# FFN down projection by seven products of halves (Strassen) in place of eight, in blocks of 512 features

## Chip, core and metric

The kernel runs on one core of one Trainium2 chip. The metric is device time in microseconds of one execution, lower is better; three runs of the kernel before are shown. The engines are TensorE (PE in the rows; PEld is its weight load), VectorE (DVE), ScalarE (ACT), GpSimd (POOL) and SyncE (SP), which here issues the loads and stores.

## What is computed

One step of a decoder layer for a prompt of 1024 tokens and 32 sample tokens, D_MODEL 1024, D_FF 4096: a combined input projection, three groups of heads (dilated attention, mLSTM, HGRN2), an output projection, an MLP and a final norm. The change is in the MLP:

```
x = x + mix.astype(x.dtype) @ w_out
u = rmsnorm(x, g_ffn) @ w_up
x = x + jnp.square(jax.nn.relu(u)) @ w_down
...
y = rmsnorm(x, g_final)
```

All matrices are float32. Where the kernel wants float32 accuracy from TensorE it splits each operand into a high part (rounded to the engine's fp32r format by a copy on ACT) and a low part (the operand less its high part), and adds three products: low × high, high × low, high × high. The helper `product` (lines 340 to 342) issues the three matmuls for each slice of 128 of the contraction.

## The kernel before

The program is written by hand engine by engine in phases (a, b, c, e, f1, f2, g). What an engine does, and in which order, is the order of the code; engines meet at semaphores, each with a running count. Phase g is the MLP after its norm. x1 holds the running sum in SBUF (eight tiles of 128 prompt tokens and one tile for the sample tokens), XH and XL the normalised and transposed input in two parts.

Phase g before runs over 16 blocks (NBLK) of 256 features (NF = 2 slices of 128):

- `hidden_piece`: six up pieces per block. A piece is one slice of 128 features by a third of the tokens (TG = 352 columns), 8 slices of the contraction × 3 = 24 matmuls of 352 columns.
- Relu on DVE (line 2496), square (2452) and high part (2454) on ACT, low part (2486) on DVE: UH and UL.
- Down: 16 products (8 token tiles × 2 halves of the output columns), each 2 slices × 3 = 6 matmuls of 512 columns into one of four PSUM banks, and one product for the sample tokens (`product_by_columns`, line 350, from raw float32). DVE adds each to x1 (line 2506).
- Weights: SP loads pieces of 512 KB (line 2087), ACT makes the high part (2091), DVE the low part (2095). POOL has nothing to do in phase g.

At the start of phase g, DVE waits for `x1_in`, which counts the loads of g_final among others: SP issues one load of g_final for the prompt (line 2379) and four small ones for the sample tokens (2381), then the weights. In the last block the tiles are finished one after the other: `final(i)` (lines 2476 to 2481) takes ACT's sum of squares and square root, a reciprocal and one pass over the tile on DVE, then SP stores it (2387). Pieces 0 and 1 of the first block are already done in phase f2; the first pieces' PSUM banks let PE do two more before it needs the first relu.

Of the kernel before, what the change touches and what calls it, by code (L numbers as in the profile page):

```python
# [39 lines left out]
P = 128  # L40
D = 1024
# [110 lines left out]
def program(nc, i_, o_):  # L152

    ctx = ExitStack()
    with ctx:
# [78 lines left out]
        R_up = [place("R_up0", 12288, 4096, F32R), place("R_up1", 16384, 4096, F32R)]  # L234
        R_down = place("R_down", 0, 4096, F32R)
        R_stage = place("R_stage", 4096, 2048)
        R_upos = place("R_upos", 7168, 704)
        R_raw = [place(f"R_raw{n}", at, 1024) for n, at in enumerate((6144, 8576, 9600, 10624))]
        R_ur = place("R_ur", 11648, 2 * NS)
        R_xr = place("R_xr", 51840, KD * NS)  # L240
        R_usq = place("R_usq", 7872, 704)
        R_u = place("R_u", 47616, 4224, F32R)
# [3 lines left out]
        R_junk = place("R_junk", 12288, 1024)  # L246
# [1584 lines left out]
        def phase_e_sync(sp):  # L1831
            load_key_chunks(sp, (6,))
            load_caches(sp, (6, 7))
            stream_values(sp)
            sp.wait_ge(ov_psum, 1)
            load_chunks(sp, 0, KD)
# [215 lines left out]
        FB = 256  # L2052
        NF = FB // P
        NBLK = DFF // FB
        wup = i_["w_up"][0].rearrange("(c k p) n -> c p k n", k=4, p=P)
# [7 lines left out]
        UP_CHUNKS, DOWN_CHUNKS = {}, {}  # L2063
        for b in range(NBLK):
            UP_CHUNKS[b] = len(CHUNKS)
            for c in range(2):
                high = 2048 * c
                CHUNKS.append((at(R_up[b % 2], high), at(R_up[b % 2], high + 1024), wup[c, :, :, b * FB:(b + 1) * FB],
                               at(R_stage, c * 1024) if b else at(R_first, c * 1024)))
            DOWN_CHUNKS[b] = len(CHUNKS)  # L2070
            for f in range(NF):
                high = 2048 * f
                CHUNKS.append((at(R_down, high), at(R_down, high + 1024), wdn[NF * b + f],
                               R_raw[2 * (b % 2) + f]))
        chunk_in = [sem(f"chunk_in{n}") for n in range(8)]
        d_psum = sem("d_psum")
        ND = 2 * NCH + 1
        def load_chunks(sp, first, last):
            for m in range(first, last):
                b, n = divmod(m - UP_CHUNKS[0], 4)  # L2080
                if n < 2 and b >= 2:
                    sp.wait_ge(chunk_split, NW + m - 3)
                if n >= 2 and b >= 2:
                    sp.wait_ge(d_psum, ND * (b - 1))
                src = CHUNKS[m][2]
                dst = CHUNKS[m][3] if len(src.shape) == 2 else CHUNKS[m][3].rearrange("p (k n) -> p k n", k=src.shape[1])
                sp.dma_start(dst, src).then_inc(chunk_in[m % 8], 16)
# [200 lines left out]
        def phase_f2_act(act):  # L2288
            for i in range(NTILE + 2):
# [8 lines left out]
                if i >= 2:  # L2298
# [6 lines left out]
                    if j in (3, 5):  # L2305
                        chunk_high_part(act, UP_CHUNKS[0] + j // 4)

        def phase_f2_dve(dve):
# [12 lines left out]
            for i in range(NTILE + 2):  # L2321
# [11 lines left out]
                if i >= 2:  # L2333
# [65 lines left out]
        def u_bank(U):  # L2399
            return U + 4 if U < 2 else U % 4  # L2400
# [178 lines left out]
```

## Time and profile before

| | |
|---|---|
| runs, us | 1560.49, 1556.29, 1560.10 |
| median, us | 1560.1 |
| profiled execution, span from first to last instruction, us | 1556.7 |
| busy in the span, us | PE 1498.3, PEld 1318.1, DVE 852.5, ACT 479.9, POOL 206.3 |
| phase g, us of the span | from about 812 to the end |
| granted TensorE clock, mean | 0.990 |

The span stands beside the runs' times: the profiled execution's span is 3.4 us under their median; no other time is given for that execution. Busy is the time in which an engine has an instruction in work. PE's matmuls overlap one another, so its busy time is longer than the pitch at which they follow. The granted clock is a share of 2.4 GHz; 0.50 is the lower level, 1.2 GHz.

### The profile page before, as it was taken

The numbers are of one execution on the slowest core, as the hardware profiler recorded it, in microseconds if no ns is written. First come the engines' busy times: TensorE is split into PE (matmuls) and PEld (weight loads), VectorE is DVE, ScalarE is ACT, GpSimd is POOL, SyncE is SP. The second block draws the span as 40 slices with busy tenths as digits, with TensorE's granted clock in tenths as the row PEclk, the third lists the DMA queues.
The fourth block names the chain that finished last, engine by engine and source line by source line (L and its number), as shares of the span: only waits on it lengthen the run. The fifth ranks groups of instructions, "written<-read, shape, count | busy, mean of one in ns | idle before, by whom it ended". The sixth has DMA issues, their size and how long they took to land.

```text
span 1556.7 us, 27891 instructions
## 1 busy us (share of the span) xinstructions
PE 1498.3 (96%) x11634; PEld 1318.1 (85%) x11634; DVE 852.5 (55%) x1729; ACT 479.9 (31%) x943; POOL 206.3 (13%) x298
## 2 busy tenths in 40 slices
PE   6999999999998998989999999999999999999997
PEld 4989899899996666858888899988899988899986
DVE  6864554668844777653455544444544444544446
ACT  6343222232213676432222222121222121222123
POOL 2212222889400000013000000000000000000000
PEclk9999999999998999999999999999999999999999
DMA  7422105522128412882103011111011111011102
GB/s 204 161 54 45 39 8 99 83 72 58 54 66 317 172 58 68 309 320 69 33 21 133 28 42 41 55 55 55 27 41 41 55 54 55 28 41 42 54 1 112
DMA packets 104559, 127.24 MB, mean 82 GB/s; under 512 B 26611, under 2 KB 78647, under 8 KB 103539
## 3 DMA queue, kind: packets, MB, share of 16 engines
q1 hardware_dynamic: 102370, 120.74, 24.9%
q0 software_dynamic: 2064, 4.72, 0.8%
q8 instruction: 93, 1.52, 0.4%
q14 instruction: 32, 0.25, 0.1%
HBM read 111.17 MB, written 18.98 MB: 84 GB/s over the span
## 4 chain that ended last, share of the span: by engine, by line
PE 89%; DVE 5%; ACT 2%; issue 2%; DMA 1%; SPq 1%; POOL 0%; DVEq 0%; ACTq 0%
PE PS L340 22%; PE PS L342 22%; PE PS L341 21%; PE PS L1644 2%; PE PS L1665 2%; PE PS L2204 2%; PE PS L2206 2%; PE PS L2205 2%; PE PS L1684 2%; PE PS L1918 2%; PE PS L350 1%; PE PS L1928 1%; PE PS L1484 1%; DVE R_att L1747 1%; DMA R_cache<-in_cache_attn_v 1%
## 5 line engine op out<-in xcount | busy, mean ns | idle before, releaser
L340 PE MATMUL PS<-x_high,R_up 128*128 128x352 f32 x768 | 249.6, 325 | 0.6 <-DVE R_upos L2496 0.6
L2506 DVE TENSOR_TENSOR R_x<-R_x,PS 128x512 f32<-128x512 f32 (+1 forms) x272 | 182.0, 671 | 123.7 <-PE PS L342 117.9
L342 PE MATMUL PS<-x_high,R_up 128*128 128x352 f32 x768 | 247.7, 322 | 0.0
L341 PE MATMUL PS<-x_low,R_up 128*128 128x352 f32 x768 | 246.8, 321 | 0.0
L2452 ACT ACTIVATE R_usq<-R_upos 128x352 f32<-128x352 f32 x96 | 47.8, 498 | 552.4 <-issue 365.1
L340 PE MATMUL PS<-R_down,R_u 128*128 128x512 f32 x512 | 202.2, 395 | 0.5 <-DVE R_u L2486 0.5
L342 PE MATMUL PS<-R_down,R_u 128*128 128x512 f32 x512 | 201.6, 394 | 0.0
L341 PE MATMUL PS<-R_down,R_u 128*128 128x512 f32 x512 | 201.1, 393 | 0.0
L2496 DVE TENSOR_SCALAR R_upos<-PS 128x352 f32<-128x352 f32 x96 | 50.3, 525 | 247.9 <-PE PS L342 242.8
L340 PEld LDWEIGHTS PS<-x_high,R_up 128*128 128x128 f32 x768 | 144.1, 188 | 7.0 <-issue 7.0
L341 PEld LDWEIGHTS PS<-x_low,R_up 128*128 128x128 f32 x768 | 144.7, 188 | 0.0
L342 PEld LDWEIGHTS PS<-x_high,R_up 128*128 128x128 f32 x768 | 144.5, 188 | 0.0
L340 PE MATMUL PS<-xn_high,R_w 128*128 128x352 f32 x384 | 126.6, 330 | 3.1 <-ACT R_hscr L730 2.0
L341 PE MATMUL PS<-xn_low,R_w 128*128 128x352 f32 x384 | 123.8, 322 | 2.0 <-issue 2.0
L340 PE MATMUL PS<-R_w,xn_low 128*128 128x256 f32 x432 | 125.5, 291 | 0.0
L342 PE MATMUL PS<-xn_high,R_w 128*128 128x352 f32 x384 | 124.1, 323 | 0.0
L341 PE MATMUL PS<-R_w,xn_high 128*128 128x256 f32 x432 | 122.7, 284 | 0.0
L342 PE MATMUL PS<-R_w,xn_high 128*128 128x256 f32 x432 | 122.2, 283 | 0.0
L342 PEld LDWEIGHTS PS<-R_down,R_u 128*128 128x128 f32 x512 | 96.1, 188 | 22.8
L340 PEld LDWEIGHTS PS<-R_down,R_u 128*128 128x128 f32 x512 | 96.1, 188 | 22.5 <-issue 1.2
L341 PEld LDWEIGHTS PS<-R_down,R_u 128*128 128x128 f32 x512 | 96.3, 188 | 21.8
L601 POOL TENSOR_TENSOR R_w<-R_wstage,R_w 128x1024 fp32r<-128x1024 f32 x29 | 74.8, 2582 | 174.6 <-ACT R_w L596 174.6
(390 smaller groups left out, 2613.1 us busy)
## 6 DMA issues: line engine op xcount, KB each, us to landing
R_raw<-in_w_down SPq DMA_DIRECT2D x32, 512.0 KB, 4.3
R_stage<-in_w_up SPq DMA_DIRECT2D x30, 512.0 KB, 3.8
R_wstage<-in_w_in SPq DMA_DIRECT2D x28, 512.0 KB, 4.3
R_cache<-in_cache_attn_v SPq DMA_DIRECT2D x56, 256.0 KB, 9.2
R_cache<-in_cache_attn_k SPq DMA_DIRECT2D x28, 256.0 KB, 5.9
R_cache<-in_cache_attn_k SPq DMA_DIRECT2D x7, 1024.0 KB, 9.4
bias_by_distance_copies<-bias_by_distance POOLq DMA_DIRECT2D x1, 4608.0 KB, 27.8
queries_and_keys<-R_spill SPq DMA_DIRECT2D x24, 176.0 KB
```

Source lines behind the costliest of these rows:

```text
L340: pe.matmul(out, ll, rh, start=(k == 0), stop=False)
L341: pe.matmul(out, lh, rl_, start=False, stop=False)
L342: mm = pe.matmul(out, lh, rh, start=False, stop=(k == n - 1))
L601: pool.tensor_tensor(parts_at(m)[1], wst[stage_of[m]], parts_at(m)[0].bitcast(F32), ALU.subtract)\
L1644: mm = pe.matmul(PS[:, 2 * h2 + c // 512, 0:min(512, nk - c)], aqk[part, hp, i * P:(i + 1) * P], aqk[part, 4 + hp, c:min(c + 512, nk)], st ...
L1665: t = pe.transpose(PS[:, 4 + gid % 2, (k - k0) * P:(k - k0 + 1) * P], PB[(2 * p + h2) % 6][:, k * P:(k + 1) * P], ident[:, :])
L1684: mm = pe.matmul(PS[64 * h2:64 * h2 + 64, 6 + p % 2, 0:P], va[:, k, 2 * hp + h2, 0:E], PT[h2][:, k, :], start=(k == 0), stop=(k == i))
L1918: t = pe.transpose(PS[:, b, a * P:(a + 1) * P], cache[4 * g + b][k][:, a * P:(a + 1) * P], ident[:, :])
L2204: pe.matmul(out, XL[:, k, ts], WOH[:, k, ns], start=(k == 0), stop=False)
L2452: act.activation(u_sq[U % 2], u_pos[U % 2], ACT.Square).then_inc(u_squared, 1)
L2496: dve.tensor_scalar(u_pos[U % 2], PS[:, u_bank(U), 0:TG], 0.0, None, ALU.max).then_inc(u_relu, 1)
L2506: dve.tensor_tensor(part, part, PS[:, 4 + j % 4, 0:w], ALU.add).then_inc(d_taken, 1)
```

## The change

The down projection of a block is done by Strassen's scheme in Winograd's form: the token halves, the feature halves and the output column halves make 2 × 2 matrices of quarters, and seven products of quarters (or of sums of quarters) take the place of eight. For that, a block has 512 features (NF = 4, NBLK = 8): twelve up pieces, the sample's product over four slices, then seven steps P1, P2, P6, P7, P5, P3, P4. A step multiplies a left operand (512 tokens × 256 features) by a right one (256 features × 512 columns): four products of six matmuls. Some steps add to a bank that holds an earlier one (P6 on P1, P7 on P6, P3 on P5), and DVE adds each product to one or two of x1's quarters (`ADDED_TO`), 32 additions of 512 columns per block.

The operands: `LEFT` and `RIGHT` name them. Sums of quarters (S_1, S_3, S_4 on the left, T_1 to T_4 on the right) are made in place, by POOL; s2 by DVE. ACT makes all high parts, DVE the left low parts and P6's right one, POOL the other right low parts and those of the up weights. There are two buffers of each operand (`ua`, `wb`). U and the raw weights stay in float32 in SBUF.

```
-        FB = 256
-        NF = FB // P
-        NBLK = DFF // FB
+        NF = 4
+        NUP = DFF // P
+        NBLK = NUP // NF
...
+        P1, P2, P6, P7, P5, P3, P4 = STEPS = range(7)
+        LEFT = {P1: q11, P2: q12, P6: s2, P7: q21, P5: q11, P3: q12, P4: q22}
+        RIGHT = {P1: w11, P2: w21, P6: t2, P7: w12, P5: w11, P3: w22, P4: w21}
+        OPENS = (P1, P2, P5, P4)
+        SECOND_BANKS = (P2, P5, P3)
+        ADDED_TO = {P1: [(0, 0)], P2: [(0, 0)], P6: [(0, 1)], P7: [(1, 0), (1, 1)], P5: [(1, 1)], P3: [(0, 1)], P4: [(1, 0)]}
...
+        def operand_free(eng, b, k):
+
+            G = 7 * b + k
+            if G >= 2:
+                pb, pk = divmod(G - 2, 7)
+                eng.wait_ge(d_psum, product_index(pb, pk, 3) + 1)
...
+            load_chunk(sp, KD + 2)
+            load_chunk(sp, KD + 3)
+            raw_rows(0, 0)
+            raw_rows(0, 1)
             for j in range(4):
                 sp.dma_start(g_sample[32 * j:32 * j + 32],
...
+            def step(b, k):
+                pe.wait_ge(dve_split, dve_count(b, k, "right" if k == P6 else "left"))
+                if k != P6:
+                    pe.wait_ge(right_split, 6 * b + POOL_LOWS.index(k) + 1)
+                (uh, ul), (wh, wl) = ua[(7 * b + k) % 2], wb[(7 * b + k) % 2]
+                for p in range(4):
+                    if k == P1 and p == 3:
+                        pe.wait_ge(d_taken, ND * b + 1)
+                    elif k == P1 and b:
+                        pe.wait_ge(d_taken, product_index(b - 1, P4, p) + 1)
+                    if k == P2:
+                        pe.wait_ge(u_relu, NU * b + NU - 3 + p)
+                    if k in (P6, P7, P5, P3, P4):
+                        pe.wait_ge(d_taken, product_index(b, {P6: P1, P7: P6, P5: P2, P3: P5, P4: P7}[k], p) + 1)
+                    out, ts = PS[:, product_bank(k, p), :], slice(p * P, (p + 1) * P)
+                    for f in range(2):
+                        pe.matmul(out, ul[:, f, ts], wh[:, f, :], start=(f == 0 and k in OPENS), stop=False, skip_group_check=True)
+                        pe.matmul(out, uh[:, f, ts], wl[:, f, :], start=False, stop=False, skip_group_check=True)
+                        mm = pe.matmul(out, uh[:, f, ts], wh[:, f, :], start=False, stop=(f == 1), skip_group_check=True)
+                    mm.then_inc(d_psum, 1)
...
+                pool.wait_ge(d_psum, ND * b + 1)
+                pool.wait_ge(right_split, 6 * b + POOL_LOWS.index(P2) + 1)
+                pool.tensor_tensor(w11, w12, w11, ALU.subtract).then_inc(pool_sums, 1)
+                pool.wait_ge(pool_sums, sums_count(b, T_1))
+                pool.tensor_tensor(t2, w22, w11, ALU.subtract).then_inc(pool_sums, 1)
+                pool.tensor_tensor(w12, w22, w12, ALU.subtract).then_inc(pool_sums, 1)
+                pool.wait_ge(pool_sums, sums_count(b, T_2))
+                pool.tensor_tensor(w21, w21, t2, ALU.subtract).then_inc(pool_sums, 1)
+                pool.wait_ge(s2_ready, b + 1)
+                pool.wait_ge(dve_split, dve_count(b, P2, "left"))
+                pool.tensor_tensor(q11, q11, s2, ALU.add).then_inc(pool_sums, 1)
+                right_low_part(b, P7)
+                pool.tensor_tensor(q12, q12, s2, ALU.subtract).then_inc(pool_sums, 1)
+                right_low_part(b, P5)
+                if not last:
+                    up_low(NF * b + 6)
+                right_low_part(b, P3)
+                right_low_part(b, P4)
...
-            dve.wait_ge(x1_in, 16 * 18)
+            dve.wait_ge(x1_in, 16 * 17)
...
+                for p in range(4):
+                    added(b, P4, p)
+                    if last:
+                        if p == 0:
+                            dve.wait_ge(x1_in, 16 * 18)
+                        final(LAST_TILES[p])
+            for i in LAST_TILES[4:]:
+                final(i)
```

`right_low_part(b, k)` on POOL waits for ACT's high part of the same operand and subtracts it; `left_low_part` does the same on DVE. `added(b, k, p)` waits for the product and adds it. The load of g_final for the prompt now goes out after the last up piece.

SP at the start of phase g: SP's rows before, from the loads of phase f2 on. R_row and R_x take g_final, R_raw w_down, R_stage w_up.

```order
L2236 DMA R_x<-in_c_token_sum 128x128
L2238 DMA R_x<-in_x_sample 32x256 x4
L2379 DMA R_row<-in_g_final 128x1024 [waits norm_split,op_psum]
L2381 DMA R_x<-in_g_final 32x256 x4
L2087 DMA R_raw<-in_w_down 128x1024 x2
L2087 DMA R_stage<-in_w_up 128x4x256 x2
```

The same place on SP now:

```order
L2221 DMA R_x<-in_c_token_sum 128x128
L2223 DMA R_x<-in_x_sample 32x256 x4
L2071 DMA R_stage<-in_w_up 128x8x128 [waits norm_split,op_psum]
L2071 DMA R_stage<-in_w_up 128x8x128
L2428 DMA R_raw<-in_w_down 128x1024 x4
L2437 DMA R_x<-in_g_final 32x256 x4
```

Two loads of w_up and four of w_down moved ahead of the four small loads of g_final, for which DVE's first wait in phase g stands; the large load of g_final left this place.

POOL in one block, which had no row in this phase before: from the low part of the up weights at the end of the up pieces to the last low part of the block. R_raw holds w_down, R_wb the right operands, R_u the squared hidden values, R_s the sum s2, and R_stage in the second row the sum t2.

```order
L2616 TENSOR_TENSOR R_raw<-R_raw 128x2x512 [waits right_split,d_psum]
L2618 TENSOR_TENSOR R_stage<-R_raw 128x1024 [waits pool_sums]
L2619 TENSOR_TENSOR R_raw<-R_raw 128x2x512
L2621 TENSOR_TENSOR R_raw<-R_raw,R_stage 128x2x512 [waits pool_sums]
L2624 TENSOR_TENSOR R_u<-R_u,R_s 128x2x512 [waits dve_split,s2_ready]
L2600 TENSOR_TENSOR R_wb<-R_raw,R_wb 128x1024 [waits operand_high]
L2626 TENSOR_TENSOR R_u<-R_u,R_s 128x2x512
L2600 TENSOR_TENSOR R_wb<-R_raw,R_wb 128x1024 [waits operand_high]
L2079 TENSOR_TENSOR R_up<-R_stage,R_up 128x1024 [waits chunk_high]
L2600 TENSOR_TENSOR R_wb<-R_raw,R_wb 128x1024 [waits operand_high] x2
```

The first of these waits for the sample's product (d_psum); the four rows of R_wb are the right low parts for P7, P5, P3 and P4, in this order.

DVE at the end of the program, before: additions of the last products and the finals of the last three tiles.

```order
L2506 TENSOR_TENSOR R_x<-R_x,PS 128x512 x2
L2476 TENSOR_SCALAR stat<-stat 128x1
L2479 RECIPROCAL stat<-stat 128x1
L2481 SCALAR_TENSOR_TENSOR R_x<-R_x,stat,R_row 128x1024
L2506 TENSOR_TENSOR R_x<-R_x,PS 128x512 x2
L2476 TENSOR_SCALAR stat<-stat 128x1
L2479 RECIPROCAL stat<-stat 128x1
L2481 SCALAR_TENSOR_TENSOR R_x<-R_x,stat,R_row 128x1024
L2476 TENSOR_SCALAR stat<-stat 128x1
L2479 RECIPROCAL stat<-stat 128x1
L2481 SCALAR_TENSOR_TENSOR R_x<-R_x,stat,R_row 128x1024
```

DVE now, from the last addition on:

```order
L2659 TENSOR_TENSOR R_x<-R_x,PS 128x512
L2639 TENSOR_SCALAR stat<-stat 128x1
L2642 RECIPROCAL stat<-stat 128x1
L2644 SCALAR_TENSOR_TENSOR R_x<-R_x,stat,R_gain 128x1024
L2639 TENSOR_SCALAR stat<-stat 128x1
L2642 RECIPROCAL stat<-stat 128x1
L2644 SCALAR_TENSOR_TENSOR R_x<-R_x,stat,R_gain 128x1024
L2639 TENSOR_SCALAR stat<-stat 128x1
L2642 RECIPROCAL stat<-stat 128x1
L2644 SCALAR_TENSOR_TENSOR R_x<-R_x,stat,R_gain 128x1024
```

The finals of one tile each no longer stand between additions: six of them follow the last addition, and the finals of the sample's tile and of tiles 0 and 1 stand between the four additions of P4.

## Rows read from the trace of the kernel before

**Rows 1.** The page: busy time by engine, and the chain that ended last.
```profile
PE 1498.3 (96%) x11634; PEld 1318.1 (85%) x11634; DVE 852.5 (55%) x1729; ACT 479.9 (31%) x943; POOL 206.3 (13%) x298
...
PE 89%; DVE 5%; ACT 2%; issue 2%; DMA 1%; SPq 1%; POOL 0%; DVEq 0%; ACTq 0%
```

**Rows 2.** The chain in order of time: start, length, what (sample products).
```profile
848.67 1.00 PE PS L350 x16
...
1499.86 1.00 PE PS L350 x16
```

**Rows 3.** Waits from 795 us: waiter, releaser, us, times, longest; PE's.
```profile
PE PS L340 <- DVE R_upos L2496: 0.6, 1, 0.6
...
PE PS L340 <- DVE R_u L2486: 0.5, 1, 0.5
```

**Rows 4.** Timeline of DVE, 1208 to 1211 us: start, length, idle before.
```profile
1208.31 0.69 DVE L2506 TENSOR_TENSOR R_x<-R_x,PS 128x512 f32<-128x512 f32 x1 [0.71 <-PE PS L342]
1209.70 0.69 DVE L2506 TENSOR_TENSOR R_x<-R_x,PS 128x512 f32<-128x512 f32 x1 [0.71 <-PE PS L342]
```

**Rows 5.** Groups by line and shape, ACT and DVE: busy, mean ns.
```profile
L2091 ACT ACTIVATE R_down<-R_raw 128x1024 fp32r<-128x1024 f32 x32 | 33.4, 1045 | 0.5 <-DMA R_raw<-in_w_down 0.5
...
L2506 DVE TENSOR_TENSOR R_x<-R_x,PS 128x512 f32<-128x512 f32 x256 | 175.2, 686 | 118.5 <-PE PS L342 117.9
...
L2095 DVE TENSOR_TENSOR R_down<-R_raw,R_down 128x1024 fp32r<-128x1024 f32 x32 | 39.0, 1220 | 1.4 <-ACT R_down L2091 1.4
```

**Rows 6.** POOL's line 601: ns min/median/max, and its timeline at 152 us.
```profile
L601 POOL TENSOR_TENSOR R_w<-R_wstage,R_w x29: 2354/2396/4443, 19.7 to 431.0; 128x1024 fp32r<-128x1024 f32 x29
...
152.46 6.99 POOL L601 TENSOR_TENSOR R_w<-R_wstage,R_w 128x1024 fp32r<-128x1024 f32 x2 [4.40 <-ACT R_w L596]
```

**Rows 7.** Timelines of POOL and of DVE, 690 to 728 us.
```profile
690.33 3.50 POOL L2138 TENSOR_TENSOR x_low<-R_mixa,x_high 128x512 fp32r<-128x512 f32 x2 [256.96 <-ACT x_high L2122]
...
726.02 1.30 POOL L2138 TENSOR_TENSOR x_low<-R_x,x_high 128x512 fp32r<-128x512 f32 x1 [1.37 <-ACT x_high L2122]
...
691.17 1.52 DVE L2095 TENSOR_TENSOR R_wo<-R_x,R_wo 128x1024 fp32r<-128x1024 f32 x1 [10.40 <-ACT R_wo L2091]
...
695.44 2.01 DVE L2095 TENSOR_TENSOR R_wo<-R_x,R_wo 128x1024 fp32r<-128x1024 f32 x1
...
726.13 1.27 DVE L2331 TENSOR_TENSOR R_x<-R_x,PS 128x512 f32<-128x512 f32 x2
```

**Rows 8.** Timelines of SP, DVE and PE, 810 to 820 us.
```profile
812.10 0.35 SPq L2379 DMA_DIRECT2D R_row<-in_g_final  x1
812.49 2.96 SPq L2381 DMA_DIRECT2D R_x<-in_g_final  x4
...
817.11 0.96 DVE L2496 TENSOR_SCALAR R_upos<-PS 128x352 f32<-128x352 f32 x2 [5.09 <-DMA R_x<-in_g_final]
...
817.78 0.40 PE L340 MATMUL PS<-x_high,R_up 128*128 128x352 f32 x1 [0.61 <-DVE R_upos L2496]
```

**Rows 9.** Windows: length, busy by engine, clock, DMA share, GB/s; loads of phases b, g.
```profile
17.00:25.00 8.00, 4.86 (x22) 4.26 (x23) 7.93 (x13) 7.08 (x16) 3.33 (x1) 0.73 1.00 272
818.00:824.00 6.00, 6.00 (x39) 6.00 (x39) 3.69 (x8) 4.64 (x9) 0.00 (x0) 1.00 1.02 372
```

**Rows 10.** Windows before and after PE's idle time at 690 us (columns: rows 9).
```profile
688.50:692.50 4.00, 1.16 (x12) 0.42 (x4) 1.33 (x1) 3.43 (x5) 2.05 (x2) 1.00 0.46 184
692.50:698.00 5.50, 5.25 (x16) 4.20 (x17) 5.49 (x12) 5.50 (x8) 3.11 (x3) 0.69 0.59 188
```

**Rows 11.** Timelines of PE and DVE at the end.
```profile
1547.79 0.39 PE L342 MATMUL PS<-R_down,R_u 128*128 128x512 f32 x1
...
1549.77 0.15 DVE L2476 TENSOR_SCALAR stat<-stat 128x1 f32<-128x1 f32 x1
...
1551.58 0.15 DVE L2476 TENSOR_SCALAR stat<-stat 128x1 f32<-128x1 f32 x1
...
1552.20 1.28 DVE L2481 SCALAR_TENSOR_TENSOR R_x<-R_x,stat,R_row 128x1024 f32<-128x1024 f32 x1
```

More of the change, by code:

```diff
@@ L1835, in phase_e_sync @@
             sp.wait_ge(ov_psum, 1)
-            load_chunks(sp, 0, KD)
+            for m in range(KD):
+                load_chunk(sp, m)
         def load_caches(sp, items):
@@ new lines, in program @@
+        ND = 1 + 7 * 4
+        POOL_LOWS = (P1, P2, P7, P5, P3, P4)
+        S_3, T_1, T_2, T_3, T_4, S_1, S_4 = range(7)
+        HIGH_ORDER = [(P1, "right"), (P2, "right"), (P1, "left"), (P2, "left"), (P6, "left"), (P6, "right")] + [
+            (k, side) for k in (P7, P5, P3, P4) for side in ("right", "left")]
+        DVE_ORDER = [(P1, "left"), (P2, "left"), (P6, "left"), (P6, "right"), (P7, "left"), (P5, "left"), (P3, "left"),
+                     (P4, "left")]
+        u_psum, u_relu, u_squared = sem("u_psum"), sem("u_relu"), sem("u_squared")
@@ L2443, in phase_g_act, with right_high_part @@
+            def right_high_part(b, k):
+                operand_free(act, b, k)
+                if k in (P1, P2):
+                    raw_loaded(act, b, k)
+                if k in (P6, P7, P5, P4):
+                    act.wait_ge(pool_sums, sums_count(b, {P6: T_2, P7: T_3, P5: T_1, P4: T_4}[k]))
+                act.activation(wb[(7 * b + k) % 2][0], RIGHT[k], ACT.Copy).then_inc(operand_high, 1)
+            act.wait_ge(xs2_T, 2 * NTILE)
             for b in range(NBLK):
-                if b:
-                    act.wait_ge(d_psum, ND * b)
+                last = b == NBLK - 1
@@ L2455, in phase_g_act @@
[L2455 to L2462 removed]
+                    squared(b * NU + u)
+                    if u == (2 if b else 1):
+                        up_high(NF * b + 3 if b else 2)
@@ new lines, in phase_g_dve @@
+                high, low = wb[(7 * b + P6) % 2]
+                dve.tensor_tensor(low, t2, high.bitcast(F32), ALU.subtract).then_inc(dve_split, 1)
+                for p in range(1, 4):
+                    added(b, P2, p)
+                added(b, P6, 0)
+                left_low_part(b, P7)
+                for p in range(1, 4):
+                    added(b, P6, p)
+                added(b, P7, 0)
+                left_low_part(b, P5)
+                for p in range(1, 4):
+                    added(b, P7, p)
```

359 lines of the change are left out of this document (219 added, 140 removed).

## The prediction

> **What bounds the kernel now.** I read the page first. PE is busy 96% of the span of 1556.7 us, and the chain that ended last is 89% PE; VectorE (DVE) holds 5% [rows 1]. So time is gained by taking matmuls off PE, provided that nothing else makes PE wait. The chain in order of time then gives the period of the FFN loop: the column products of the sample tokens start at 848.67 in the first block of 256 features and at 1499.86 in the fifteenth, 14 periods of 46.51 us [rows 2]. The waits from 795 us on show that PE stood still for 0.6 and 0.5 us in all, both in the first block [rows 3]. In the steady blocks PE never waits, and the loop is worth what its matmuls are worth.
>
> One down product (one tile of 128 tokens by 512 columns, six matmuls) costs 1.39 us: DVE adds follow each other at 1208.31 and 1209.70, and each waits 0.71 us for PE [rows 4]. One matmul of 512 columns is thus 0.232 us. A block of 46.51 us is 16 × 1.393 = 22.3 of down products, 1.0 for the sample's product [rows 2] and, what is left, 23.2 for six up pieces, 3.87 each.
>
> **The change part by part.** *Products.* Two blocks of 256 features hold 32 down products. The new block of 512 features holds 7 steps × 4 = 28, of six matmuls each. Up pieces and sample products keep their number (12 pieces; 16 rather than 2 × 8 column matmuls). So each new block saves 4 × 1.393 = 5.57 us, and eight save **44.6 us**. A new block is 93.02 − 5.57 = 87.4 us: 46.4 up, 2.0 sample, 39.0 in seven steps of 5.57. The same price holds since form, operand types and pitch are the same, and the accumulation over two steps in one bank adds no matmul.
>
> *Operands of the steps.* Each step needs a left and a right operand split in two. ACT makes the high parts (1.045 us, as its 1024-column copy), DVE the left low parts (1.22 us) [rows 5], POOL the right low parts and six of the sums that come after the sample's product. POOL did nothing in this loop before. Its price for the same operation and width is 2.40 us (median; 2.35 to 4.44) [rows 6]. I set t = 0 at the sample's product, so P1 runs from 2.0 to 7.6, P2 to 13.1, P6 to 18.7, P7 to 24.3, P5 to 29.9, P3 to 35.4, P4 to 41.0.
>
> POOL's chain starts when the sample's product is out (its first sum overwrites the weights), at 2.4: its low part of the up weights is done by 0.9 (the eleventh of the twelve pieces ends at −3.9, relu and square take 1.2 with their hand-overs, ACT 1.05, POOL 2.4). Then follow T_1, T_2, T_3, T_4, S_1 and the low part for P7: six operations, 14.4 us, done at 16.8 if nothing disturbs it. What disturbs it is DVE: a POOL pair of 512 columns took 3.50 us beside DVE subtractions with both inputs in SBUF, against 1.30 for one alone, and those DVE operations took 1.52 and 2.01 in place of 1.22; beside DVE additions with one input in PSUM, POOL stayed at 1.30 and DVE at 1.27 for two [rows 7]. The 32 additions per block are of the second kind. Four DVE operations of the first kind fall into this chain (left for P2, left and right for P6, left for P7). Stretch per operation: bounds 0 (all of it on DVE's side, as in its 2.01) and 0.9 (3.50 less two of 1.30); I take 0.35 for POOL and 0.5 for DVE. P7's operand is then there at 16.8 + 1.4 + some 0.3 of hand-overs = 18.5, and PE wants it at 18.7. Next, low part for P5: two operations and one stretch on, 23.7, wanted at 24.3; for P3 28.9 against 29.9; for P4 ACT must wait for P5's end (buffer of two), 29.9 + 0.4 + 1.05, then 2.4 to 2.75: 34.1 against 35.4.
>
> DVE's chain: P1's last addition ends at 8.65, ACT's high part of s2 at 9.05, left low for P6 until 10.7, one addition until 11.4, right low for P6 until 13.1; wanted at 13.1. P7's eight additions (0.69 each, [rows 5]) and P3's left low end at 28.9, the first addition of P5 at 29.6, and P3 may start only after it: wanted at 29.9. In all DVE has 32 × 0.69 + 7 × 1.22 + 1.6 = 32 us of work in the 41 us of a down stage; it has slack, but little of it at three places. POOL's places are as tight. I charge 0.4 us of PE wait per block, **+3 us** in all; bounds 0 and 12 (below). Up weights, sums before the sample's product and P1's and P2's right parts lie under the 46 us of up pieces, and so do the loads.
>
> The Trainium skill, GPSIMD Engine Reference, section 3 (Performance versus the Vector engine), holds that ordinary elementwise work belongs on VectorE, since GpSimd takes 4497 ns for a two-input add of 2048 columns against 2293. Halved, an estimate from that page, this is 2.25 us, and POOL's chain would end 0.9 us sooner; the sum would lose most of its 3 us of waits. Against the rule's advice stands that DVE, with 32 us of 41 taken, would need 11 × 1.22 = 13 us more, above PE's 41.
>
> *Start of the loop.* DVE waits for x1_in before its first relu. Before, the transfers it waits for go out first: SP issues from 812.10, the relu starts at 817.11, PE's fifth piece at 817.78 after 0.61 us of waiting [rows 8]. Now six loads of 512 KB (two of w_up, four of w_down) go out ahead of the four small gain loads. SP needs about 0.45 us to issue each large one, then 2.96 for the small ones [rows 8]: the last is out near 817.4. Data starts about 1.1 us after the first issue. w_up with rows of 512 bytes moves at the 272 GB/s of the stage that loaded w_in in such rows, w_down at 372 [rows 9]: 1.05 MB in 3.9 and 2.1 MB in 5.6 us, so the small ones land near 823.1 and the relu follows. PE has two pieces that don't need it and stands still from 817.2 to 823.8: **+6.2 us** against now. Bounds: 819.5 if the small loads pass the large ones (last issue plus the 2 us they take now), +2.4; 825.4 with 272 GB/s for all, +8.2. The clock falls as well: after 4 us in which PE was busy for 1.2, it ran at a mean of 0.69 over 5.5 us, between its level of 1.2 GHz and that of 2.4 [rows 10], which is 1.7 us lost: **+1.8**.
>
> *End.* Before, finals (normalise and store) are spread over the last block's products; the last runs alone, at a pitch of 1.81 us (1549.77, 1551.58), and ends 5.3 us after the last matmul (1548.18; 1553.48) [rows 11]. Now tiles 4 to 7 are complete only after P4's last product, and DVE has four additions (2.7 us), eight finals of 1.81 and the sample's (about 1.0, its last operation being a quarter as wide) to do from the first product of P4 on, 1.7 us after P4's start. That ends 19.9 us after P4's start, 14.3 after PE's last matmul: **+9 us**. ACT's square of the next tile fits under each final, as now.
>
> Before's 0.5 us wait at the first down product goes. Sum: −44.6 − 0.5 + 3 + 6.2 + 1.8 + 9 = **−25.1 us**. The profiled execution has a span of 1556.7; the median of the runs is 1560.1, 3.4 above it, and I carry the difference to the median: **1535 us**.
>
> **The rivals.** (A) POOL becomes the pace of the down stage, and the kernel is slower. With price r per operation the wait is 6r − 16.3 for P7, then 2r − 5.57 each for P5 and P3. The sum without waits is −28.1, or 3.5 us per block, used up at r = 3.1 us. For it speaks a POOL pair of 6.99 us beside a DVE scan, 3.5 each [rows 6]: 4.7 + 1.4 + 1.4 = 7.5 us per block, 60 in all, 1592 us. Against it: no such scan runs here, and only one DVE operation in five has both inputs in SBUF. The Trainium skill, GPSIMD Engine Reference, section 8 (Key points), says that GpSimd shares its SBUF interfaces with VectorE and contends with instructions that have two SBUF inputs; rows 7 show that kind and its size. (B) Waits vanish and the small loads pass the large ones: −44.6 − 0.5 + 2.4 + 9, with the clock's loss halved: 1527 us. (C) The operands come late in every block by 1.5 us (r near 2.75, or DVE's three tight places each 0.5 late): 9 us more than in the sum, 1544. (D) The matmul side doesn't save (steps start with three waits, matmuls into a bank that DVE has just read are slower) by 0.1 us per product or more: 224 products, +22, 1557, no change. Nothing in the rows shows such a price; in the loop now each product has a wait too.
>
> **How the numbers follow.** The sum's case 0.58, B 0.15, C 0.18, A 0.06, D 0.03. The predicted time is the sum's. The range of 1524 to 1547 holds the sum, B and C with the bounds of start and waits. No change means within 0.3% of 1560.1, about 4.7 us, which is what this kernel's measurement can tell: faster 0.91, same 0.03, slower 0.06.
>
> **What would show it.** Period of a block 87.4 to 88.5 us between sample products; 168 matmuls per block at 0.232 us; POOL operations of 2.4 to 2.8 us; PE's waits in steps P6, P7 and P3 below 0.5 us each; one PE wait of about 6 us near 817 us, ended by DVE, whose wait a g_final load ends, and matmuls at half clock after it; 14 us from the last matmul to DVE's last operation. The prediction is wrong if POOL's mean nears 3.1 us, if PE waits in each of the seven steps, or if the relu at the start isn't held.

## The result, and the profile after

The changed kernel takes 1547.07 us (median of five runs, 1545.99 to 1550.43) against 1560.1 for the kernel before in the same session (five runs, 1555.98 to 1563.7): a ratio of 0.9931, 95% interval 0.9917 to 0.9945. It is faster by 13 us, where 25 were forecast, and lies just past the slow end of the range. The profiled execution took 1547.07 us with a span of 1545.3, which is 11.4 less than the span before.

The page after, busy time by engine and the chain that ended last; it answers to [rows 1]:

```profile
PE 1455.8 (94%) x11442; PEld 1282.2 (83%) x11442; DVE 889.2 (58%) x1635; ACT 508.8 (33%) x895; POOL 562.8 (36%) x432
...
PE 78%; DVE 11%; issue 7%; ACT 3%; DMA 1%; SPq 0%; POOL 0%; DVEq 0%; ACTq 0%
```

PE lost 42.5 us of busy time; as its matmuls overlap, that is not the saving in time, which is worked out further down. 11 points of its share of the chain went to others: DVE now holds 11%, "issue" 7%. PE no longer sets the pace alone. The chain in order of time gives the period of a block, sample product to sample product [rows 2]:

```profile
858.01 1.86 PE PS L350 x32
947.59 1.86 PE PS L350 x32
...
1485.00 1.86 PE PS L350 x32
```

Seven periods take 626.99 us: **89.57 each**, against 93.02 for two blocks before and 87.4 to 88.5 forecast. What PE waits for, from 795 us on (waiter, releaser, us in all, times, longest), answers to [rows 3]:

```profile
PE PS L2510 <- DVE R_wb L2686: 12.8, 8, 1.6
PE PS L340 <- DVE R_u L2669: 8.1, 1, 8.1
PE PS L2510 <- DVE R_x L2659: 4.6, 7, 0.7
```

The first row is step P6, which waits 1.6 us in every block for DVE's low part of its right operand. The third is P3, 0.66 us in seven blocks: DVE's first addition of P5, which stands behind P3's left low part. The second is the start of the loop. The groups by line and shape from 840 us on (count, busy, mean ns) show what became slow, against [rows 5, 6]:

```profile
L2659 DVE TENSOR_TENSOR R_x<-R_x,PS 128x512 f32<-128x512 f32 x256 | 162.7, 678 | 23.5 <-PE PS L2512 23.3
L2649 DVE TENSOR_TENSOR R_ua<-R_u,R_ua 128x1024 fp32r<-128x1024 f32 x48 | 119.8, 2495 | 0.0
...
L2686 DVE TENSOR_TENSOR R_wb<-R_stage,R_wb 128x1024 fp32r<-128x1024 f32 x8 | 22.5, 2813 | 0.0
...
L2600 POOL TENSOR_TENSOR R_wb<-R_raw,R_wb 128x1024 fp32r<-128x1024 f32 x48 | 115.1, 2398 | 42.0 <-ACT R_wb L2554 42.0
...
L2624 POOL TENSOR_TENSOR R_u<-R_u,R_s 128x1024 f32<-128x1024 f32 x8 | 27.1, 3386 | 0.0
```

DVE's additions from PSUM take 678 ns, as before. Its left low parts take 2495 ns on the mean, where the same operation took 1220. On POOL some lines take 2.4 us, as in [rows 6], and others 3.4, always the same ones. The timelines of DVE and POOL in the block that begins at 947.59 say why:

```profile
948.71 1.23 DVE L2675 TENSOR_TENSOR R_s<-R_u 128x1024 f32<-128x1024 f32 x1 [0.56 <-ACT R_u L2531]
949.86 3.42 DVE L2649 TENSOR_TENSOR R_ua<-R_u,R_ua 128x1024 fp32r<-128x1024 f32 x1
...
956.52 2.47 DVE L2649 TENSOR_TENSOR R_ua<-R_s,R_ua 128x1024 fp32r<-128x1024 f32 x1 [0.48 <-ACT R_ua L2546]
958.91 0.67 DVE L2659 TENSOR_TENSOR R_x<-R_x,PS 128x512 f32<-128x512 f32 x1
959.51 2.81 DVE L2686 TENSOR_TENSOR R_wb<-R_stage,R_wb 128x1024 fp32r<-128x1024 f32 x1
...
949.56 2.63 POOL L2616 TENSOR_TENSOR R_raw<-R_raw 128x1024 f32<-128x1024 f32 x1 [1.29 <-PE PS L350]
952.28 3.26 POOL L2618 TENSOR_TENSOR R_stage<-R_raw 128x1024 f32<-128x1024 f32 x1
955.50 2.41 POOL L2619 TENSOR_TENSOR R_raw<-R_raw 128x1024 f32<-128x1024 f32 x1
957.87 3.37 POOL L2621 TENSOR_TENSOR R_raw<-R_raw,R_stage 128x1024 f32<-128x1024 f32 x1
961.19 3.39 POOL L2624 TENSOR_TENSOR R_u<-R_u,R_s 128x1024 f32<-128x1024 f32 x1
```

Read them as one queue. s2 begins before POOL's first sum and takes 1.23; that sum begins 0.4 before s2 ends, and takes 2.63. P2's left low part begins at 949.86, inside POOL's first sum, which ends at 952.19; it ends at 953.28, 1.09 later. POOL's second sum, begun at 952.28, takes 3.26 in place of 2.40, most of the 1.0 us until then. So it goes on: P6's left low part ends 1.08 after POOL's 955.50 one, P6's right one 1.08 after the 957.87 one, and POOL's next instruction is about 1 us longer each time. The addition between them, with an input in PSUM, takes 0.67 beside a running POOL instruction. The reading: **a DVE operation with both inputs in SBUF and a POOL operation never run together; the later one waits until the whole instruction of the other is done.** It holds throughout: in the loop of the changed kernel 63 such DVE operations began inside a POOL instruction, and every one ends 1.08 or 1.09 after that instruction does. The Trainium skill, SBUF — State Buffer, section "SBUF: two separate sides", says just that: the port pair that both use is an exclusive lock held for a full instruction, no split of bandwidth, and a DVE instruction with two SBUF inputs takes part in it against a GpSimd instruction that reads SBUF. The rows agree, with waits of 1.4 to 2.3 us on DVE's side and 0.9 to 1.0 on POOL's.

The trace of before had it too. In [rows 7] the DVE operation of 695.44 ends at 697.45, which is 1.08 after the end of this one of POOL, itself not stretched at all:

```profile
695.09 1.28 POOL L2138 TENSOR_TENSOR x_low<-R_x,x_high 128x512 fp32r<-128x512 f32 x1 [1.25 <-ACT x_high L2122]
```

The operation of 691.17 there ends at 692.69, 1.1 after the first half of POOL's pair would end if it took 1.28.

The start of the loop, SP, DVE and PE [rows 8], and then windows (us, busy by engine, clock, DMA share, GB/s):

```profile
811.60 1.01 SPq L2071 DMA_DIRECT2D R_stage<-in_w_up  x2
812.66 3.04 SPq L2428 DMA_DIRECT2D R_raw<-in_w_down  x4
815.74 1.82 SPq L2437 DMA_DIRECT2D R_x<-in_g_final  x4
...
824.11 1.81 DVE L2669 TENSOR_SCALAR R_u<-PS 128x352 f32<-128x352 f32 x4 [12.59 <-DMA R_x<-in_g_final]
...
824.78 0.63 PE L340 MATMUL PS<-x_high,R_up 128*128 128x352 f32 x1 [8.11 <-DVE R_u L2669]
```

```profile
820.00:824.00 4.00, 0.00 (x0) 0.00 (x0) 0.00 (x0) 0.00 (x0) 0.00 (x0) 0.50 0.58 219
824.00:828.00 4.00, 3.22 (x11) 3.25 (x12) 1.81 (x4) 3.28 (x6) 1.37 (x1) 0.50 0.00 0
828.00:832.00 4.00, 4.00 (x21) 4.00 (x20) 0.52 (x1) 0.37 (x2) 1.01 (x1) 0.73 0.36 105
```

The small loads land at 824.1 (823.1 forecast), PE's fifth piece starts 7.0 us later than before, and the granted clock is at its level of 1.2 GHz until 828, 0.73 on the mean until 832. The end, PE and DVE [rows 11]:

```profile
1527.70 0.39 PE L2512 MATMUL PS<-R_wb,R_ua 128*128 128x512 f32 x1
...
1538.97 1.28 DVE L2644 SCALAR_TENSOR_TENSOR R_x<-R_x,stat,R_gain 128x1024 f32<-128x1024 f32 x1
...
1540.79 1.28 DVE L2644 SCALAR_TENSOR_TENSOR R_x<-R_x,stat,R_gain 128x1024 f32<-128x1024 f32 x1
```

From the last matmul's end (1528.09) to DVE's last (1542.07) it is 14.0 us, against 5.3 before. So the span's −11.4 divides into +7.0 at the start, +8.7 at the end, and −27.1 from the fifth piece to the last matmul (730.4 before, 703.3 now), where −44.6 with 3 of waits and 1.8 of clock had been forecast.

### The profile page after: what moved, and what is told of

It reads as the page before. It is cut to its first block, busy times and chain, and to the rows that moved or that the text cites. A ratio compares the mean times of both kernels' runs of the same rounds, so it can differ in the third digit from the quotient of the medians.

```text
span 1545.3 us, 27564 instructions
## 1 busy us (share of the span) xinstructions
PE 1455.8 (94%) x11442; PEld 1282.2 (83%) x11442; DVE 889.2 (58%) x1635; ACT 508.8 (33%) x895; POOL 562.8 (36%) x432
## 4 chain that ended last, share of the span: by engine, by line
PE 78%; DVE 11%; issue 7%; ACT 3%; DMA 1%; SPq 0%; POOL 0%; DVEq 0%; ACTq 0%
PE PS L340 15%; PE PS L341 14%; PE PS L342 14%; DVE R_x L2659 4%; PE PS L2510 4%; PE PS L2512 3%; PE PS L2511 3%; PE PS L1644 2%; PE PS L1665 2%; PE PS L2188 2%; PE PS L2190 2%; PE PS L2189 2%; PE PS L1684 2%; PE PS L1919 2%; PE PS L350 1%
## 5 line engine op out<-in xcount | busy, mean ns | idle before, releaser
L2669 DVE TENSOR_SCALAR R_u<-PS 128x352 f32<-128x352 f32 x96 | 50.0, 524 | 305.0 <-PE PS L342 292.4
L2079 POOL TENSOR_TENSOR R_up<-R_stage,R_up 128x1024 fp32r<-128x1024 f32 x30 | 78.8, 2626 | 356.8 <-ACT R_up L2075 356.8
L2510 PE MATMUL PS<-R_wb,R_ua 128*128 128x512 f32 x448 | 179.9, 402 | 17.5 <-DVE R_wb L2686 12.8
L2659 DVE TENSOR_TENSOR R_x<-R_x,PS 128x512 f32<-128x512 f32 x256 | 162.7, 678 | 23.5 <-PE PS L2512 23.3
L2511 PE MATMUL PS<-R_wb,R_ua 128*128 128x512 f32 x448 | 174.8, 390 | 0.0
L2512 PE MATMUL PS<-R_wb,R_ua 128*128 128x512 f32 x448 | 174.7, 390 | 0.0
L2531 ACT ACTIVATE R_u<-R_u 128x352 f32<-128x352 f32 x96 | 47.6, 498 | 352.5 <-DVE R_u L2669 352.5
L2600 POOL TENSOR_TENSOR R_wb<-R_raw,R_wb 128x1024 fp32r<-128x1024 f32 x48 | 115.1, 2398 | 42.0 <-ACT R_wb L2554 42.0
L2510 PEld LDWEIGHTS PS<-R_wb,R_ua 128*128 128x128 f32 x448 | 84.0, 187 | 51.7 <-DVE R_wb L2686 16.2
```

The costliest lines, as they stand in the source:

```text
L2079: eng.tensor_tensor(CHUNKS[m][1], CHUNKS[m][3], CHUNKS[m][0].bitcast(F32), ALU.subtract).then_inc(chunk_split, 1)
L2510: pe.matmul(out, ul[:, f, ts], wh[:, f, :], start=(f == 0 and k in OPENS), stop=False, skip_group_check=True)
L2511: pe.matmul(out, uh[:, f, ts], wl[:, f, :], start=False, stop=False, skip_group_check=True)
L2512: mm = pe.matmul(out, uh[:, f, ts], wh[:, f, :], start=False, stop=(f == 1), skip_group_check=True)
L2531: act.activation(part, part, ACT.Square).then_inc(u_squared, 1)
L2600: pool.tensor_tensor(low, RIGHT[k], high.bitcast(F32), ALU.subtract).then_inc(right_split, 1)
```

## The experiments

The theory is the lock above. Its first rival was that DVE simply has too much to do or has it in a bad order; the second, that POOL is too slow. All times are medians; where no interval is given, it is a single run. The period is the mean of the seven.

**1. Small gain loads first.** Start only.

```
+            for j in range(4):
+                sp.dma_start(g_sample[32 * j:32 * j + 32], ...).then_inc(x1_in, 16)
             load_chunk(sp, KD + 2)
...
             raw_rows(0, 1)
-            for j in range(4):
-                sp.dma_start(g_sample[32 * j:32 * j + 32], ...).then_inc(x1_in, 16)
```

> The four small g_final loads that DVE waits for go out ahead of the six large loads at the start of the MLP phase; nothing else changes. Theory (the small loads are stuck behind 3 MB): DVE's first relu starts near 816 us in place of 824, PE's wait of 8.1 us there goes, the clock no longer drops, and the time falls by 8 to 10 us, to about 1538. Rival (the wait is for something else, such as the large loads themselves): the relu stays near 824 and the time at 1547.

1536.67 us, ratio to before 0.985 (0.9826 to 0.9874), 10.4 below the changed kernel. PE's wait at the start is gone; the period stays at 89.56. Before still had 0.6 us of wait there, so the change's start cost 9.8 in all: 7.0 of PE's later start and, as the rest, 2.8 of clock. The windows above give 2.7 for it: 3.22 × 0.50 + 4.00 × 0.27.

**2. P6's right low part ahead of P2's first addition on DVE.**

```
                 left_low_part(b, P6)
-                added(b, P2, 0)
                 dve.wait_ge(operand_high, high_count(b, P6, "right"))
...
                 dve.tensor_tensor(low, t2, high.bitcast(F32), ALU.subtract).then_inc(dve_split, 1)
+                added(b, P2, 0)
```

> In DVE's order the right low part for P6 moves ahead of the first addition of P2 (0.6 us); nothing else changes. Theory (DVE is the pace of the down stage): PE's wait at P6 falls from 1.6 us by 0.6 us in each of eight blocks, the time by 4 to 5 us, to about 1542. Rival (GpSimd's chain or a cost at the step's start on PE is the pace): no change, 1547.

1547.3 us, ratio 0.992 (0.99 to 0.9941): no change, P6's wait still 1.6. The low part started earlier but took 3.40 in place of 2.81 and ended at the same place, at the end of POOL's instruction plus 1.1. The rival that DVE's order sets the pace, with 1542 expected, fell here.

**3. POOL's six sums cut to 8 of 512 columns** (most of each sum is left out). **4. The six sums as copies with one input, full width** (the sums are left out). One of the six:

```
-                pool.tensor_tensor(w11, w12, w11, ALU.subtract).then_inc(pool_sums, 1)
+                pool.tensor_tensor(w11[:, :, 0:8], w12[:, :, 0:8], w11[:, :, 0:8], ALU.subtract)...   (3)
+                pool.tensor_copy(w11, w12).then_inc(pool_sums, 1)                                     (4)
```

> The six sums that GpSimd makes after the sample's product are cut to the first 8 of 512 columns, so that part of the computation is left out; all waits stay. Theory (GpSimd's two-input work stretches DVE's subtractions from 1.22 to 2.5 us and DVE so is late): DVE's left low parts fall below 1.8 us on the mean, PE's waits for DVE at P6 and P3 go, the block's period falls from 89.6 to 87.4 us and the time by 17 us, to about 1530. Rival (PE's steps are long in themselves): the period stays above 89 us.

> The same six sums on GpSimd become copies of one of their operands at full width, so the sums are left out but GpSimd still works on 1024 columns each time, with one input. Theory (it is two SBUF inputs on both engines that collide): DVE's low part for P2, 3.4 us beside the sums, falls to about 1.3 beside the copies; mean of DVE's left low parts below 1.8 us, PE's waits at P6 and P3 go, time about 1530. Rival (any GpSimd work beside DVE stretches it): the low part for P2 stays above 2 us and PE's waits stay over half of what they are.

1523.45 and 1522.84 us; the period is 86.5 in both, and PE's wait at P6 is gone. Both are 7 us below the 1530 expected, as the expectation for 3 put the period at 87.4. With short sums P2's left low part takes 1.24. With copies the timelines of DVE and of POOL show:

```profile
946.39 2.06 DVE L2649 TENSOR_TENSOR R_ua<-R_u,R_ua 128x1024 fp32r<-128x1024 f32 x1
...
946.09 1.29 POOL L2616 COPY R_raw<-R_raw 128x1024 f32<-128x1024 f32 x1 [1.28 <-PE PS L350]
947.43 1.92 POOL L2618 COPY R_stage<-R_raw 128x1024 f32<-128x1024 f32 x1
949.30 1.04 POOL L2619 COPY R_raw<-R_raw 128x1024 f32<-128x1024 f32 x1
```

DVE ends at 948.45, 1.07 after the copy it met, and the next copy takes 1.92, not 1.04. So it is not POOL's second input that shuts DVE out, as my expectation for 4 had it (about 1.3 us beside a copy): a copy does it too. The rival there held for the low part but not for PE's waits, which went: a copy alone takes 1.04 us, a sum 2.40.

The two runs also come near what the matmuls alone need. DVE's additions of P1 in experiment 3 follow PE at 1.36:

```profile
951.03 0.69 DVE L2659 TENSOR_TENSOR R_x<-R_x,PS 128x512 f32<-128x512 f32 x1 [0.67 <-PE PS L2512]
952.39 0.69 DVE L2659 TENSOR_TENSOR R_x<-R_x,PS 128x512 f32<-128x512 f32 x1 [0.67 <-PE PS L2512]
```

A step without a wait is thus 5.44, and P2, P6 and P7 begin 5.44 apart there (952.19, 957.63, 963.07). The seven steps together take 38.75, still 0.67 more than 7 × 5.44, at the starts of P1 and P3. Without that a block would take 85.8.

**5. Each sum as two instructions of half the width.**

```
-                pool.tensor_tensor(w11, w12, w11, ALU.subtract).then_inc(pool_sums, 1)
+                for h in range(2):
+                    ins = pool.tensor_tensor(w11[:, h], w12[:, h], w11[:, h], ALU.subtract)
+                ins.then_inc(pool_sums, 1)
```

> Each of GpSimd's six sums becomes two instructions of 512 columns. Theory (one instruction at a time holds a way into SBUF that both engines need: DVE's operation with two SBUF inputs waits for GpSimd's running instruction to end, and the other way round): DVE's low part for P2 falls from 3.4 us to about 2.3 (1.2 of waiting at most, then 1.1), and the wait at P6 becomes shorter; GpSimd's chain gets longer by 0.2 us per sum, so P7 waits in its place and the time stays within 5 us of 1547. Rival (the two engines share bandwidth while both run): the low part for P2 stays at 3.4 us, as the same columns move.

1558.25 us, period 90.80. DVE's side came as the lock has it, and not as a shared bandwidth would, which would have left P2's left low part at 3.42:

```profile
951.14 2.32 DVE L2661 TENSOR_TENSOR R_ua<-R_u,R_ua 128x1024 fp32r<-128x1024 f32 x1
```

P6's two take 1.96 and 1.72, and P6 no longer waits. But DVE now gets in between POOL's halves each time, POOL's six operations up to P7's low part end 19.3 us after their start instead of 17.4, and PE waits at P7 for 20.3 us in eight blocks. The wait moved from the one engine to the other; the time was expected within 5 us of 1547, and is 11 above it.

**6. POOL's T_4 held until P6's right low part is done**, with the order of 2. **7. The same, P7's low part ahead of S_1, and the third up weight's behind P4's. 8. The same with the start of 1.**

```
                 pool.wait_ge(pool_sums, sums_count(b, T_2))
+                pool.wait_ge(dve_split, dve_count(b, P6, "right"))
                 pool.tensor_tensor(w21, w21, t2, ALU.subtract).then_inc(pool_sums, 1)
+                right_low_part(b, P7)                                          (7, 8)
                 pool.wait_ge(s2_ready, b + 1)
...
-                right_low_part(b, P7)                                          (7, 8)
...
-                if not last:
-                    up_low(NF * b + 6)                                         (7, 8)
                 right_low_part(b, P3)
                 right_low_part(b, P4)
+                if not last:
+                    up_low(NF * b + 6)                                         (7, 8)
```

> DVE makes the right low part for P6 ahead of P2's first addition, and GpSimd holds T_4 back until it is done; nothing else. Theory (the shared way in is full from the sample's product to P7, whoever goes first): PE's wait at P6 goes, and a wait of 1.5 to 2 us at P7 for GpSimd's low part comes in its place; time within 3 us of 1547. Rival (DVE's lateness at P6 alone is the cost): the wait at P6 goes and none comes, 13 us less, 1534.

> As the run before, and GpSimd makes the right low part for P7 before S_1, and the low part of the up weights after that for P4. The same work, in the order in which the steps want it. Theory: waits at P6, P7 and P3 nearly go, the block's period falls from 89.6 to 86.5 to 87 us, the time by 20 to 24 us, to about 1525. Rival (the down stage has too much work for the shared way in, whatever the order): the period stays above 88.5.

> The run before with the four small g_final loads ahead of the large ones. Theory: both gains add up, 1547 less 22 less 10, about 1515. Rival (the early loads are late for the first steps when DVE starts earlier): above 1522.

1551.94; 1545.84, ratio 0.9917 (0.9902 to 0.9933); 1537.53, ratio 0.9859 (0.9836 to 0.9881). In 6 P6's right low part takes 1.22 and P6 doesn't wait, but P7 does, 2.26 us a block; the time is 5 us above 1547, where at most 3 was expected. In 7 neither waits, but P5 does, 2.27: DVE's and POOL's timelines there

```profile
967.92 2.27 DVE L2650 TENSOR_TENSOR R_ua<-R_u,R_ua 128x1024 fp32r<-128x1024 f32 x1 [0.42 <-ACT R_ua L2546]
...
966.69 2.42 POOL L2627 TENSOR_TENSOR R_u<-R_u,R_s 128x1024 f32<-128x1024 f32 x1
969.06 5.73 POOL L2600 TENSOR_TENSOR R_wb<-R_raw,R_wb 128x1024 fp32r<-128x1024 f32 x2
```

have P5's low part behind S_4 and behind P5's left low part. My expectation of 1525 for 7 failed, and 8 is no better than 1. In these orders the wait only moves on: from POOL's start, just after the sample's product, the work that excludes itself fills the time until P7 or P5. In the changed kernel POOL's low part for P7 already ends at 966.94, 19.4 on the prediction's clock (t = 0 at 947.52), after the 18.7 at which P7 was to begin; the lateness of P6 hides it.

**9. An earlier start for POOL, alone.** The sample's product, which POOL's first sum waits for, goes ahead of the twelfth up piece.

```
                     hidden_piece(pe, b, u)
-                sample_product(b)
+                    if u == NU - 2:
+                        sample_product(b)
...
-                    if u in (7, 10) and not last:
-                        up_high(NF * b + 4 + (u - 7) // 3)
+                    if u in (7, 9) and not last:
+                        up_high(NF * b + 4 + (u - 7) // 2)
```

> Change: the sample's product is issued before the twelfth up piece instead of behind it, and ACT's high part of the next block's second up weight one piece earlier, so that POOL's chain of sums starts about 3.7 us earlier against PE; the order on DVE and the start of the loop stay. Theory (POOL's and DVE's operations with both inputs in SBUF shut each other out, and the total of such work from the sample's product to P7 is what comes late): P2's left low part no longer meets a sum at its worst place, POOL's chain runs ahead of PE, the waits at P7, P5, P3 stay away; P6's wait is left at 1 us or less, since its right low part stands behind P1's additions, which don't move. Period 86.8 to 88.2 us against 89.57, 11 to 22 us off the time: 1525 to 1536. Rival (what comes late is DVE's own order in the first two steps, whenever POOL starts): P6's wait stays at 1.6 us and the period at 89 or more, 1543 to 1547.

1574.7 us, ratio 1.0096 (1.0076 to 1.0115): slower than before, and both expectations missed it. P6's wait is gone, but PE waits 4.0 us per block at P1's fourth product, whose bank waits for DVE's addition of the sample's product. Experiment 11 shows the place.

**10. Earlier start and an order for the lock.** Start of 1, the edit of 9, and

```
                 pool.tensor_tensor(t2, w22, w11, ALU.subtract).then_inc(pool_sums, 1)
+                pool.wait_ge(dve_split, dve_count(b, P2, "left"))
                 pool.tensor_tensor(w12, w22, w12, ALU.subtract).then_inc(pool_sums, 1)
...
                 pool.wait_ge(s2_ready, b + 1)
-                pool.wait_ge(dve_split, dve_count(b, P2, "left"))
+                pool.wait_ge(dve_split, dve_count(b, P6, "right"))
                 pool.tensor_tensor(q11, q11, s2, ALU.add).then_inc(pool_sums, 1)
                 right_low_part(b, P7)
-                pool.tensor_tensor(q12, q12, s2, ALU.subtract).then_inc(pool_sums, 1)
                 right_low_part(b, P5)
+                pool.tensor_tensor(q12, q12, s2, ALU.subtract).then_inc(pool_sums, 1)
```

with the third up weight's low part behind P4's, the order of 2, and P5's first addition ahead of P3's left low part on DVE.

> Change: the small gain loads first, the sample's product early, POOL's T_3 held until P2's left low part is done and S_1 until P6's right low part is done, P6's right low part ahead of P2's additions, the low part for P5 before S_4, the low part of the third up weight behind P4's, one addition of P5 ahead of P3's left low part. Theory (mutual exclusion): with both POOL's earlier start and an order in which neither engine stands behind the other, all operands arrive in time: PE waits below 0.3 us per block, period 86.5 to 87, start 10 us shorter: 1512 to 1522 us, 25 to 35 us below the changed kernel. Rival (the work with both inputs in SBUF is too much for the stage in any order, as the wait's moves from P6 to P7 to P5 suggest): a wait of 2 us appears at P3 or P4, period 88.5 or more, 1530 to 1538, no better than the gain loads alone.

**1512.6 us** (five runs, 1511.7 to 1519.21), ratio to before 0.9709 (0.9685 to 0.9734): 34.5 us below the changed kernel, 46 below before, as the theory had it. The chain in order of time, all that PE waits for from 795 us on, and the timelines of DVE and POOL:

```profile
842.70 1.86 PE PS L350 x32
...
1448.68 1.86 PE PS L350 x32
```

```profile
PE PS L2510 <- DVE R_ua L2651: 1.5, 8, 0.2
```

```profile
936.26 1.23 DVE L2677 TENSOR_TENSOR R_s<-R_u 128x1024 f32<-128x1024 f32 x1 [0.56 <-ACT R_u L2532]
937.40 1.22 DVE L2651 TENSOR_TENSOR R_ua<-R_u,R_ua 128x1024 fp32r<-128x1024 f32 x1
...
938.70 2.42 POOL L2621 TENSOR_TENSOR R_raw<-R_raw 128x1024 f32<-128x1024 f32 x1 [2.60 <-DVE R_ua L2651]
```

The period is 86.57, as short as without the sums. POOL stands idle for 2.6 us on purpose while s2 and P2's left low part run in 1.2 us each, and PE waits 0.2 us in a block.

**11. As 10 without the hold before T_3. 12. As 10 with the sample's product back behind the twelfth piece.**

```
-                pool.wait_ge(dve_split, dve_count(b, P2, "left"))              (11)
                 pool.tensor_tensor(w12, w22, w12, ALU.subtract).then_inc(pool_sums, 1)
...
-                    if u == NU - 2:                                            (12)
-                        sample_product(b)                                      (12)
+                sample_product(b)                                              (12)
```

> Change against the eighth order (e10, 1512.6 us): only POOL's wait for P2's left low part ahead of T_3 is taken out, so that POOL's four sums of the weights run back to back. Theory (mutual exclusion for a whole instruction): T_3 and T_4 shut out s2 and P2's left low part on DVE, 3.3 us each in place of 1.2, the addition of the sample's product stands behind them, and P1's fourth product, which needs its bank, waits 3.5 to 4 us in each block as with the early chain alone: period 90 to 90.6, 1538 to 1546. Rival (the early start of the chain made the gain and the wait is incidental, POOL being only earlier without it): 1508 to 1518.

> Change against the eighth order (e10, 1512.6 us): only the sample's product goes back behind the twelfth up piece; POOL's holds and all orders stay. Theory (total of the excluding work from the sample's product to P7 or P5 is too much when it starts 3.8 us later): POOL's sums start 3.8 us later, the holds push T_3, S_1 and the low part for P7 further, and PE waits 2 to 4 us per block at P6, P7 or P5: period 88.5 to 90.5, 1528 to 1545. Rival (order and holds alone make the gain): 1511 to 1518.

1557.31, ratio 0.9985 (0.9969 to 1.0), and 1530.44, ratio 0.981 (0.9786 to 0.9834). Neither half makes the gain alone: 12 is 6 us below experiment 1 and has P6's wait of 1.6 back, a little under the 2 to 4 expected (period 88.65). 11 is slower than the 1538 to 1546 expected, though its mechanism is as told; DVE, POOL and then windows:

```profile
943.48 3.27 DVE L2676 TENSOR_TENSOR R_s<-R_u 128x1024 f32<-128x1024 f32 x1 [0.56 <-ACT R_u L2532]
946.67 3.35 DVE L2650 TENSOR_TENSOR R_ua<-R_u,R_ua 128x1024 fp32r<-128x1024 f32 x1
949.95 0.41 DVE L2679 TENSOR_TENSOR R_x<-R_x,PS 128x256 f32<-128x256 f32 x1
...
943.28 2.39 POOL L2620 TENSOR_TENSOR R_raw<-R_raw 128x1024 f32<-128x1024 f32 x1
945.63 3.32 POOL L2622 TENSOR_TENSOR R_raw<-R_raw,R_stage 128x1024 f32<-128x1024 f32 x1
```

```profile
946.00:950.40 4.40, 0.45 (x2) 0.03 (x1) 4.40 (x4) 0.00 (x0) 2.95 (x1) 1.00 0.00 0
950.40:952.40 2.00, 1.98 (x5) 1.60 (x6) 1.75 (x3) 0.00 (x0) 0.00 (x0) 0.55 0.04 8
952.40:954.00 1.60, 1.60 (x5) 1.22 (x5) 0.69 (x1) 0.77 (x1) 0.00 (x0) 0.50 0.00 0
```

T_3 and T_4 shut out s2 and P2's left low part, and the 0.4 us addition behind them is 4 us late for PE. After that wait the granted clock is near its 1.2 GHz level for 3.6 us: 2.0 × 0.45 + 1.6 × 0.50, or 1.7 us of work lost. The period is 91.91, 5.3 above that of 10: the wait of 4.0 and the clock's 1.7, less some 0.5 that 10 loses at the start of P7 and 11 does not. The clock is what the expectation lacked.

## Why the prediction failed, point by point

- **Operand waits (+3): the step that failed.** I took the stretch in [rows 7] as a sharing, 0.5 us per DVE operation and 0.35 on POOL. It is exclusion, and its size is what is left of the other engine's instruction: 1.27 us on the mean for DVE's left low parts, 1.59 for P6's right one, 1.0 on POOL. The DVE operations of [rows 7] met POOL instructions of half the width, 1.30 us alone, and lost 0.3 and 0.8; beside one of 2.40 they lose up to 2.2. The second of them did not stand beside the pair of 3.50, as the prediction has it, but beside the single instruction of 695.09. In the terms of the prediction's clock (t = 0 at 947.52) P6's left low part ended at 11.5 instead of 10.7, and its right one at 14.8 instead of 13.1. The seven steps of a block take 41.81 from P1's first matmul to the next up piece, where 7 × 5.44 would be 38.08. So the waits cost 3.73 × 8 = 29.8 us, ten times the 3 forecast: 17.4 in the rows of waits, the rest, as far as it is traced, at the starts of steps, whose first matmuls follow at 0.28 to 0.36 in place of 0.23. (Against the period of experiment 3, which has a little of this itself, it is 24.5.) The bound of 12 us that I kept for this term was too low as well. The rule of the Trainium skill, SBUF — State Buffer, section "SBUF: two separate sides", was not weighed in the prediction. With 2.40 us of [rows 6] as the instruction met it gives, as an estimate, up to 2.4 for each DVE operation that I had at 0.5.
- **Products (−44.6):** right in kind, too small. A product takes 1.36 us, not 1.393 (pitch of DVE's additions in experiment 3), and the up pieces of a block 45.9, not 46.4. So the matmuls save 93.02 − 85.84 = 7.18 per block, 57.4 in all. That these 12.8 us hid almost half of the first error is luck: with the forecast saving and the measured waits the change would have gained nothing.
- **Start (+6.2 and +1.8):** right in mechanism, 7.0 and 2.8 measured, by experiment 1.
- **End (+9):** 8.7, with finals at the pitch of 1.81 as told.
- The terms as measured: −57.4 + 29.8 + 9.8 + 8.7 and −0.5 for before's wait give −9.6, against −11.4 of the span; the 1.8 between them (P3 waits in seven blocks only, and the first and last block otherwise) is not divided further. The medians differ by 13.0, since the span of before lies 3.4 under the median of its runs and that of after 1.8.
- **The rivals.** C (1.5 us late in every block) named DVE's tight places and came nearest, with 1544; but the waits were more than twice its 12 us, and the cheaper matmuls brought the time back to it. A's condition wasn't met: POOL's six operations take 17.4 us, 2.9 each, below 3.1. B's no waits and D's dear matmuls aren't there; the matmuls are cheaper.

## What to carry to other kernels

Work moved to GpSimd is not free cover for VectorE: count every VectorE operation with both inputs in SBUF and every GpSimd sum, subtraction or copy in the same stretch as one queue, and price a meeting at up to the whole of the other's instruction. Where the sum fits, give the queue an order: start GpSimd earlier where its inputs allow it, and let it stand still for the VectorE operation whose successor PE waits for. Here the two together were worth 24 us (1536.67 to 1512.6); the order with the late start gave 6, and the early start alone cost 28.

## What the runs showed of the hardware that was not expected

A GpSimd copy with one input shuts out VectorE as a two-input sum does (2.06 us for an operation of 1.2, beside a copy of 1.29 us). A wait of PE of 4.0 us was followed by 3.6 us at a granted clock of 0.50 to 0.55, while after P6's waits of 1.6 us the windows of the changed kernel show 1.00:

```profile
962.70:964.70 2.00, 2.00 (x10) 1.65 (x9) 2.00 (x5) 0.10 (x1) 2.00 (x2) 1.00 0.38 100
```

The six matmuls of a product follow at 0.227 us in experiment 3 and at 0.232 in the loop before, both at a clock of 1.00; no run tells why.
